# Gate one-hots made 512 elements at a time, two tokens innermost, with the third term on ScalarE

## What is computed

```
idx = i1 * N_KEYS + i2                    # 8 heads x 16 choices = 128 pairs per token
g = jax.nn.softmax(top_s, axis=-1)
u_sel = jnp.take(u_tab, idx, axis=0)
h = jnp.einsum('bthkd,btd->bthk', u_sel, xb)
a = (jax.nn.gelu(h.astype(jnp.float32)) * g).astype(xb.dtype)
return jnp.einsum('bthk,bthkd->btd', a, jnp.take(v_tab, idx, axis=0))
```

## Time and profile before

| | |
|---|---|
| median of 3 runs | 1876.62 us (1874.97 to 1881.18) |
| the profiled execution | 1873.83 us, span 1872.0 us |
| TensorE busy | 1701.3 us, 91% |
| VectorE busy | 1269.0 us, 68% |
| ScalarE busy | 816.0 us, 44% |
| GpSimd busy | 562.8 us, 30% |

### The profile page before, as it was taken

How to read it: one execution, slowest core, us unless ns; L and a number is a source line. 1 busy time by engine, 2 the same in 40 slices (tenths; PEclk the granted TensorE clock), 3 DMA queues, 4 the chain that set the end, 5 groups by cost and what they waited for, 6 DMA issues and landing times.

```text
span 1872.0 us, 33695 instructions
## 1 busy us (share of the span) xinstructions
PE 1701.3 (91%) x13542; PEld 1630.7 (87%) x13542; DVE 1269.0 (68%) x2746; ACT 816.0 (44%) x1337; POOL 562.8 (30%) x430
## 2 busy tenths in 40 slices
PE   4999988899999999999889978787788899999999
PEld 4999977689998888899889977777788899999999
DVE  7666665556667566566699997778888755555555
ACT  4544433545455553344344433333333344444443
POOL 1111132211111320100369977776767300000000
PEclk9999998899999999999999989999999999999999
DMA  3555533235555434345335533333333455555554
GB/s 131 180 184 187 179 138 124 89 126 186 187 180 163 141 120 130 120 146 185 111 126 179 172 122 123 115 113 123 112 116 114 135 180 176 175 179 180 176 175 134
DMA packets 77963, 277.59 MB, mean 148 GB/s; under 512 B 9048, under 2 KB 10456, under 8 KB 77808
## 3 DMA queue, kind: packets, MB, share of 16 engines
q1 hardware_dynamic: 77808, 275.43, 45.7%
HBM read 274.35 MB, written 1.05 MB: 147 GB/s over the span
## 4 chain that ended last, share of the span: by engine, by line
PE 33%; DVE 24%; ACT 4%; issue 3%; POOL 0%; DVEq 0%; ACTq 0%
PE ps L752 33%; DVE WL L322 5%; DVE BIG L1211 4%; ACT WH L479 4%; DVE XT L1701 3%; DVE XT L1700 3%; DVE XT L1699 2%; DVE BIG L1626 1%; DVE BIG L1621 1%; DVE BIG L1624 1%; DVE BIG L1619 1%; DVE BIG L1622 1%; DVE BIG L1658 0%; DVE BIG L1664 0%; POOL MS L375 0%
## 5 line engine op out<-in xcount | busy, mean ns | idle before, releaser
L322 DVE TENSOR_TENSOR WL<-RAW,WH 128x1024 fp32r<-128x1024 f32 x446 | 547.3, 1228 | 432.6 <-ACT WH L479 432.4
L479 ACT ACTIVATE WH<-RAW 128x1024 fp32r<-128x1024 f32 x510 | 538.1, 1057 | 590.6 <-PE ps L752 588.2
L752 PE MATMUL ps<-HH,WH 128*128 128x256 f32 x2320 | 685.0, 295 | 37.7 <-DVE HL L1211 17.8
L752 PE MATMUL ps<-HL,WH 128*128 128x256 f32 x2320 | 668.1, 288 | 0.0
L752 PE MATMUL ps<-HH,WL 128*128 128x256 f32 x2320 | 667.1, 288 | 0.0
L752 PEld LDWEIGHTS ps<-HH,WH 128*128 128x128 f32 x2320 | 457.0, 197 | 52.9 <-issue 30.7
L752 PEld LDWEIGHTS ps<-HL,WH 128*128 128x128 f32 x2320 | 457.2, 197 | 1.0 <-issue 1.0
L752 PEld LDWEIGHTS ps<-HH,WL 128*128 128x128 f32 x2320 | 456.9, 197 | 0.0
L752 PE MATMUL ps<-GH,WH 128*128 128x256 f32 x1440 | 415.2, 288 | 8.4 <-DVE GL L1211 8.4
L752 PE MATMUL ps<-GL,WH 128*128 128x256 f32 x1440 | 407.8, 283 | 0.0
L752 PE MATMUL ps<-GH,WL 128*128 128x256 f32 x1440 | 407.5, 283 | 0.0
(11 more groups left out here) (245 smaller groups left out, 1682.1 us busy)
## 6 DMA issues: line engine op xcount, KB each, us to landing
RAW<-wall SPq DMA_DIRECT2D x510, 512.0 KB, 3.5
B<-rel SPq DMA_DIRECT2D x4, 768.0 KB, 5.2
DEC<-con SPq DMA_DIRECT2D x4, 384.0 KB, 4.1
XT<-xt SPq DMA_DIRECT2D x4, 256.0 KB, 3.3
out<-XT SPq DMA_DIRECT2D x4, 256.0 KB, 2.1
NMASK<-con SPq DMA_DIRECT2D x1, 192.0 KB
CS<-con SPq DMA_DIRECT2D x1, 128.0 KB
SN<-con SPq DMA_DIRECT2D x1, 128.0 KB
```

The costliest lines, as they stand in the source:

```text
L322: ins = eng.tensor_tensor(wl, RAW[:, b % NRAW, :], wh.bitcast(F), ALU.subtract)
L479: act.activation(WH[:, b % NSPLIT, :], RAW[:, b % NRAW, :], ACT.Copy).then_inc(s_hi, 1)
L752: return pe.matmul(o, l, r, start=start, stop=stop, skip_group_check=True)
```

## The change

The one-hots get a new layout: tokens go in pairs, and a pair's two values for one key are adjacent. IREP holds each key number twice, and RB is bf16, so VectorE compares a whole group in one instruction: 512 elements, with the row of four tokens' i1 or i2 repeated along the keys. onehot(i2) goes to a new buffer OH2, from which two more instructions multiply out the first and second term. ScalarE multiplies out the third with four copies that take RB3, an f32 column, as their scale; it does so after WH of the next round. GpSimd has nothing left in the stage. TensorE reads its operands with a step of two elements. rows() casts straight into RB, without GB16. IREP and OH2 are new; s_oh tells that OH2 is written, and s_pp now tells that ScalarE has read it.

```
-            RB = sb("RB", [128, 5, T], F, ph)
-            IOTB = sb("IOTB", [128, 128], B16, ph)[:, :]
+            RB = sb("RB", [128, 4, T], B16, ph)
+            RB3 = sb("RB3", [128, T], F, ph)
+            IREP = sb("IREP", [128, 128, 2], B16, ph)
+            OH2 = sb("OH2", [128, 2, 512], B16, ph)
-        ONEH = XB.rearrange("p (s a t i) -> p s a t i", s=2, a=4, t=4)
+        ONEH = XB.rearrange("p (s a w i t) -> p s a w i t", s=2, a=4, w=2, t=2)
+        OH2 = OH2[:, :, :].rearrange("p s (w i t) -> p s w i t", w=2, t=2)
...
-            def weighted(i):
-                if i >= 2:
-                    pool.wait_ge(s_bt, i - 1)
-                for t in range(4):
-                    j = 4 * i + t
-                    ins = pool.tensor_scalar(ONEH[:, i % 2, 3, t, :], IOTB, RB[:, 1, j:j + 1], RB[:, 4, j:j + 1],
-                                             ALU.is_equal, ALU.mult)
-                ins.then_inc(s_pp, 1)
...
+            def weighted(i):
+
+                act.wait_ge(s_oh, i + 1)
+                if i >= 2:
+                    act.wait_ge(s_bt, i - 1)
+                for t in range(4):
+                    j = 4 * i + t
+                    ins = act.activation(ONEH[:, i % 2, 3, t // 2, :, t % 2], OH2[:, i % 2, t // 2, :, t % 2], ACT.Copy,
+                                         scale=RB3[:, j:j + 1])
+                ins.then_inc(s_pp, 1)
...
                     high(UP + c + 2)
+                    if c - 1 in QUAD_AT:
+                        weighted(QUAD_AT[c - 1])
...
-                        ins = mm(o[:, c128(t)], ONEH[:, i % 2, 0, t, :], ONEH[:, i % 2, p + 1, t, :], p == 0 and t == 0,
-                                 p == 2)
+                        ins = mm(o[:, c128(t)], ONEH[:, i % 2, 0, t // 2, :, t % 2], ONEH[:, i % 2, p + 1, t // 2, :, t % 2],
+                                 p == 0 and t == 0, p == 2)
...
-                    done(dve.tensor_copy(GB16, GT_[:, 0, cols]))
-                    dve.wait_ge(s_route, nr)
-                    done(dve.tensor_copy(RB[:, 2 + k, cols], GB16))
+                    done(dve.tensor_copy(RB[:, 2 + k, cols], GT_[:, 0, cols]))
...
-                done(dve.tensor_copy(GB16, GT_[:, 0, cols]))
-                dve.wait_ge(s_route, nr)
-                done(dve.tensor_copy(RB[:, 4, cols], GB16))
+                done(dve.tensor_copy(RB3[:, cols], GT_[:, 0, cols]))
...
             def one_hots(i):
+                s = i % 2
+
+                def row(r):
+                    return RB[:, r, 4 * i:4 * i + 4].rearrange("p (w t) -> p w t", t=2).unsqueeze(2).to_broadcast(
+                        [128, 2, 128, 2])
+
+                keys = IREP[:, :, :].unsqueeze(1).to_broadcast([128, 2, 128, 2])
                 if i == 0:
                     dve.wait_ge(s_route, nr)
                 elif i >= 2:
                     dve.wait_ge(s_bt, i - 1)
-                for t in range(4):
-                    j, o = 4 * i + t, ONEH[:, i % 2, :, t, :]
-                    dve.tensor_scalar(o[:, 0, :], IOTB, RB[:, 0, j:j + 1], None, ALU.is_equal)
-                    dve.tensor_scalar(o[:, 1, :], IOTB, RB[:, 1, j:j + 1], RB[:, 2, j:j + 1], ALU.is_equal, ALU.mult)
-                    ins = dve.tensor_scalar(o[:, 2, :], IOTB, RB[:, 1, j:j + 1], RB[:, 3, j:j + 1], ALU.is_equal,
-                                            ALU.mult)
-                ins.then_inc(s_pd, 1)
+                    dve.wait_ge(s_pp, i - 1)
+                tt(OH2[:, s], row(1), keys, ALU.is_equal).then_inc(s_oh, 1)
+                tt(ONEH[:, s, 0], row(0), keys, ALU.is_equal)
+                dve.wait_ge(s_oh, i + 1)
+                tt(ONEH[:, s, 1], OH2[:, s], row(2), ALU.mult)
+                tt(ONEH[:, s, 2], OH2[:, s], row(3), ALU.mult).then_inc(s_pd, 1)
```

More of the change, by code:

```diff
@@ L164 @@
 TURN_SLOT = {27: 0, 42: 1}
-ROUTE_STEPS = 1 + 5 * 48 + 2 * (1 + 11 + 2 + 10)
 def build(nc, wall, par, con, xt, rel, keys, out):
@@ L245, in build @@
             BIG = sb("BIG", [128, 128 * T], F, ph)
-            RB = sb("RB", [128, 5, T], F, ph)
-            IOTB = sb("IOTB", [128, 128], B16, ph)[:, :]
+            RB = sb("RB", [128, 4, T], B16, ph)
+            RB3 = sb("RB3", [128, T], F, ph)
+            IREP = sb("IREP", [128, 128, 2], B16, ph)
+            OH2 = sb("OH2", [128, 2, 512], B16, ph)
             GT_ = sb("GT_", [128, 2, T], F, ph)
-            GB16 = sb("GB16", [128, 128], B16, ph)[:, :]
         BIG3 = BIG[:, :].rearrange("p (c t) -> p c t", t=T)
         XB = XT[:, :, :].rearrange("p k t -> p (k t)").bitcast(B16)
-        ONEH = XB.rearrange("p (s a t i) -> p s a t i", s=2, a=4, t=4)
+        ONEH = XB.rearrange("p (s a w i t) -> p s a w i t", s=2, a=4, w=2, t=2)
+        OH2 = OH2[:, :, :].rearrange("p s (w i t) -> p s w i t", w=2, t=2)
         top = 128 * T
@@ L308, in build @@
             "s_xin", "s_xn", "s_qt", "s_pqk", "s_scm", "s_sc", "s_route", "s_gt", "s_rtr"))
-        s_pd, s_pp, s_bt, s_mm, s_mc, s_gel, s_tmg, s_xo = (sem(n) for n in (
-            "s_pd", "s_pp", "s_bt", "s_mm", "s_mc", "s_gel", "s_tmg", "s_xo"))
+        s_oh, s_pd, s_pp, s_bt, s_mm, s_mc, s_gel, s_tmg, s_xo = (sem(n) for n in (
+            "s_oh", "s_pd", "s_pp", "s_bt", "s_mm", "s_mc", "s_gel", "s_tmg", "s_xo"))
         def wait_low(eng, b):
@@ L453, in pool_program @@
             power(5)
-            def weighted(i):
-                if i >= 2:
-                    pool.wait_ge(s_bt, i - 1)
-                for t in range(4):
-                    j = 4 * i + t
-                    ins = pool.tensor_scalar(ONEH[:, i % 2, 3, t, :], IOTB, RB[:, 1, j:j + 1], RB[:, 4, j:j + 1],
-                                             ALU.is_equal, ALU.mult)
-                ins.then_inc(s_pp, 1)
-            for b in range(PQ + 3, WP):
+            for b in range(PQ + 3, UP + ROUTED):
                 low_if_mine(b + 2)
[L467 to L470, removed]
         def scalar_program(act):
@@ L1724, in vector_program @@
             dve.wait_ge(d_iota, 16)
-            done(dve.tensor_copy(IOTB, IOTA))
+            done(dve.tensor_copy(IREP[:, :, :], IOTA.unsqueeze(2).to_broadcast([128, 128, 2])))
             for l in range(3, 16):
@@ L1752, in vector_program @@
             rows(1)
-            assert nr == ROUTE_STEPS
             for c in range(ROUTED, 128):
```

## The result

The changed kernel takes 1817.6 us (median of 4 runs, 1814.09 to 1821.72) against 1876.3 before (the three runs named above and a fourth, 1876.01): ratio 0.968, 95% interval 0.966 to 0.971. The forecast was 1819. The profiled execution took 1814.09 us, its span 1812.3.

What follows compares the result with a forecast made beforehand. A loop of VectorE and ScalarE waiting for each other bounds the gate stage. From the profiled 1873.83 us, minus 55 (gate stage) and 3 (routing) is 1816; the timed median lies 2.8 above: 1819, range 1806 to 1852.

Steps and rivals of the forecast that it cites:

- The loop: Gate stage: VectorE and ScalarE wait for each other; a period of 13 rounds falls from 58.7 to 50.0 us.
- A: Gate-stage round with one-hots and a product in the next round: from 5.50 to 4.32 us, seven per period.
- B: Gate-stage round with one-hots but no product next: from 3.76 to 2.68 us, three per period.
- C: Gate-stage round without one-hots, product next: from 2.96 to 3.90 us, three per period.
- Four instructions in place of twelve: VectorE's one-hots: four 512-element two-input instructions take 1.36 us, where the twelve took 2.54.
- the ends: VectorE's four instructions: half the f32 time per element taken (1.31 us); a quarter, 0.81 us, was the other end.
- The rival: VectorE's four instructions stream at the f32 rate and cost 2.42 us: slower, 1885 us; chance 0.14.
- ScalarE's copies: Third term on ScalarE: four copies after WH, near 0.30 us each, 1.31 until the last ends; bounds 0.94 and 1.64.
- the new chain: Product, L701 (L714 before), WH, four ScalarE copies, twelve matmuls, next product: 3.90 us, ruling rounds without one-hots.
- ran beside everything: GpSimd's 4 x 1.02 us for the third term ran beside everything, waited for once, before the first group.
- The routing: Fewer casts while routing ends: 0.8 us in the second half, at most one 2.87 us GpSimd turn in the first; 3 taken.
- TensorE's operands with gaps: Gate-stage matmuls reading with a one-element gap cost nothing, the twelve staying at 0.66 us; slow-load rival 1.44, chance 0.05.

Runs made afterwards that it cites:

- e5: Changed kernel with only ScalarE's order altered: Gelu, WH, third term's copies, then L701; 1783.57 us.
- e1: Changed kernel with one token innermost in place of a pair, so the row operand is one element repeated 128 times; 1885.25 us.
- e8: Changed kernel with ScalarE's third-term copies before L701 only in rounds that have a product to wait for, otherwise behind WH; 1796.11 us.
- e2: Changed kernel with the third term on GpSimd again, as four one-input multiplications of 128 elements from OH2; 1848.53 us.
- e4: Changed kernel with ScalarE's third-term copies moved behind the Gelu and before L701 in every round; 1818.09 us.
- e7: Kernel before the change with only WH moved ahead of L714 on ScalarE; 1805.19 us.

## Why the prediction was right

- *What bounds the stage.* Right. The loop with its three kinds of round was read from the earlier trace rows, and each part of it moved as the sum said: A 4.32 forecast and 4.30 measured, B 2.68 and 2.65, C 3.90 and 3.98; the stage 55 us shorter, and 54.9. e5 shows the loop: taking WH out of it, without touching any instruction, ends it.
- *Four instructions in place of twelve.* Right in mechanism and size, 1.36 us forecast and 1.34 measured. The term that could have failed was the rate of an operand that no row showed, and e1 shows what it hung on. The choice between the ends, half the f32 time per element, came from a cast in the earlier trace rows and was a weaker ground than its success suggests: that cast has one source. The rival's time was exact (1885 and 1885.25). One detail was wrong: all four instructions read a row with repeated pairs, not three of them. The rival's price had all four at the slow rate, so nothing came of it.
- *ScalarE's copies.* Right: 1.31 us forecast, 1.30 measured, and the new chain was in the forecast before any trace showed it. It was short by 0.08 us, of which 0.07 lies between the last copy and the matmuls (0.11 against 0.04). e8 puts its cost at 21 us, where the forecast had 3 x 0.94 x 6.3 = 18.
- *GpSimd.* This is where the working was thin. It said that GpSimd "ran beside everything", which holds for the kernel before, and so gave its removal no worth. In the form of e2 it does not run beside the new rounds: that costs 31 us, mainly because VectorE's instructions hold GpSimd's (4.46 us in place of 2.79). The sum came out right because the change removes GpSimd from the stage.
- *The routing.* 3 us forecast, 4.0 measured between two fixed points. The mechanism, one GpSimd turn in the first half and 0.8 us in the second, is what the rows show: two held instructions in place of three, 2.88 us less in the first half and 0.78 in the second.
- *TensorE's operands with gaps.* Right to take nothing: 0.65 us against 0.64 without gaps.
- *The sum.* 1819 for 1817.6. With 1 us less from the casts than came and 3 x 0.08 x 6.3 = 1.5 too much hoped for in kind C, the errors are small and cancel in part. That they leave 1.4 us is partly luck, since the executions of one kernel differ by more (1814.09 to 1821.72).

What the forecast did not ask is how large the gain could have been. It saw that the loop had 13.7 us of slack per period to TensorE's bound and priced a cheaper link; that WH needs no place in the loop at all was visible in ScalarE's order, where WH waits only for its block and its data (s_blk, d_raw) and never for the product ahead of it.

## What to carry to other kernels

When two engines wait for each other, write out the loop with its links and ask of each whether the next needs it: moving one instruction that needs nothing of its predecessor brought 70 us in the old kernel (1875.46 and 1805.19), more than the 58 of the whole rewrite beside it, and made the faster arithmetic worth 6.5 us in place of 68. Sort the rounds by kind before multiplying; e4 and e2 gained in one kind what they lost in another, and an average would have shown neither. On VectorE, a two-source instruction on 2-byte data with a repeated operand reached the double rate here with a pair of elements innermost and not with a single one.

## What the runs showed of the hardware that was not expected

- VectorE's instructions held GpSimd's more than the reverse: a one-input multiplication of 128 bf16 elements on GpSimd takes 0.64 us with VectorE idle, 1.01 beside VectorE's multiplications of 512 and 1.82 beside its L322, while VectorE's own grew only from 420 to 445 and 463 ns (e2). GpSimd's two-input L322 in turn held casts of 0.23 us for up to 2.31 in the routing.
- So GpSimd's mean of 838 ns in e2 is no length of the instruction. The old one, with a comparison and two scalar operands, had a mean of 1020 ns before and 1173 in e7, where VectorE hardly waits.
- TensorE's granted clock fell to 0.50 behind one wait of 2.43 us in e2 (before 1311.51) and not behind another of 2.42 (before 1295.16); in e5, where TensorE waits for nobody, it was 1.00 from 1110 to 1390 us.
